# Attention's products with the values: features first, two heads side by side, scaled by spread reciprocals

## The reference, cut to what matters

```
logits = q_lat . c_sel - slope * dist        # masked outside the picked keys
p      = softmax(logits)
o_lat  = p @ c_sel                           # (B, S, 8, 128)
o      = einsum('bshr,hrd->bshd', o_lat, w_uv)   # (B, S, 8, 64), joined to 512 columns
mix    = concat([o, mlstm_out]) @ w_out
```

## Time and profile before

| | us |
|---|---|
| median of 3 runs | 2357.65 |
| lowest, highest | 2354.97, 2359.41 |
| profiled execution, its time | 2356.38 |
| profiled execution, its span | 2354.6 |
| granted TensorE clock, mean over the span | 0.981 |

### The profile page before, as it was taken

The page is one execution under the profiler, slowest core; times in us unless marked ns, Lnnn a source line. Parts: engine busy times, 40 slices in busy tenths (PEclk is TensorE's granted clock), DMA queues, the critical chain, the costliest instruction groups (busy, mean ns, idle before and its releaser), DMA issues.

```text
span 2354.6 us, 35457 instructions
## 1 busy us (share of the span) xinstructions
PE 2254.9 (96%) x10615; PEld 1674.4 (71%) x10616; DVE 1707.5 (73%) x2859; ACT 1338.3 (57%) x1719; POOL 359.9 (15%) x231
## 2 busy tenths in 40 slices
PE   8999998889999999999999999999999999999992
PEld 3644446667755678888888877888787787888872
DVE  0387794745445667778978699787979979778797
ACT  0368723555312555656766577566757757556575
POOL 0000941200020211101201031021103103011030
PEclk9999998989999999999999999999999999999996
DMA  4100002000322967688988799687979979868795
GB/s 178 72 5 36 1 0 90 1 1 1 135 85 94 284 205 231 230 305 292 346 289 303 237 336 365 229 320 240 370 230 346 359 229 346 280 225 306 230 341 208
DMA packets 81676, 493.47 MB, mean 210 GB/s; under 512 B 12307, under 2 KB 13587, under 8 KB 30515
## 3 DMA queue, kind: packets, MB, share of 16 engines
q1 hardware_dynamic: 67344, 451.11, 52.2%
q0 software_dynamic: 12592, 38.29, 7.0%
q10 hardware_dynamic: 1686, 3.37, 0.5%
HBM read 462.31 MB, written 37.88 MB: 212 GB/s over the span
## 4 chain that ended last, share of the span: by engine, by line
PE 66%; DVE 14%; issue 11%; ACT 4%; DVEq 3%; DMA 1%; ACTq 0%; POOL 0%; POOLq 0%; SPq 0%
DVE wlo L1594 8%; PE ps L890 7%; PE ps L888 7%; PE ps L889 7%; PE ps L571 6%; PE ps L885 6%; PE ps L886 6%; PE ps L582 5%; PE ps L762 5%; PE ps L866 3%; PE ps L745 2%; DVEq L408 2%; PE ps L726 2%; ACT whi L1136 2%; PE ps L733 1%
## 5 line engine op out<-in xcount | busy, mean ns | idle before, releaser
L1594 DVE TENSOR_TENSOR wlo<-raw,whi 128x2048 fp32r<-128x2048 f32 x388 | 886.2, 2288 | 248.8 <-ACT whi L1136 205.9
L1136 ACT ACTIVATE whi<-raw 128x2048 fp32r<-128x2048 f32 x388 | 743.1, 1916 | 331.8 <-PE ps L890 331.2
L890 PE MATMUL ps<-whi,xlo 128*128 128x512 f32 x1024 | 399.7, 390 | 0.0
L889 PE MATMUL ps<-wlo,xhi 128*128 128x512 f32 x1024 | 399.6, 390 | 0.0
L888 PE MATMUL ps<-whi,xhi 128*128 128x512 f32 x1024 | 399.2, 390 | 0.0
L1904 POOL DMA_INDIRECT acc<-ysb,idx_cur x45 | 87.6, 1947 | 966.8 <-DVE ysb L1742 593.8
L889 PEld LDWEIGHTS ps<-wlo,xhi 128*128 128x128 f32 x1024 | 192.3, 188 | 40.3
L890 PEld LDWEIGHTS ps<-whi,xlo 128*128 128x128 f32 x1024 | 192.3, 188 | 40.2
L888 PEld LDWEIGHTS ps<-whi,xhi 128*128 128x128 f32 x1024 | 192.5, 188 | 39.2
L888 PE MATMUL ps<-whi,hhi 128*128 128x512 f32 x512 | 206.7, 404 | 0.0
L890 PE MATMUL ps<-whi,hlo 128*128 128x512 f32 x512 | 200.6, 392 | 0.0
(11 more groups left out here) (333 smaller groups left out, 3346.1 us busy)
## 6 DMA issues: line engine op xcount, KB each, us to landing
raw<-in_w_gu SPq DMA_DIRECT2D x260, 1024.0 KB, 6.8
raw<-in_w_dn SPq DMA_DIRECT2D x128, 1024.0 KB, 5.7
raw<-in_w_out SPq DMA_DIRECT2D x2, 2048.0 KB, 9.3
h1all<-in_x SPq DMA_DIRECT2D x4, 1024.0 KB, 8.6
hext<-h1all SPq DMA_DIRECT2D x8, 512.0 KB, 2.6
acc<-h1all SPq DMA_DIRECT2D x8, 512.0 KB, 3.6
fin<-acc SPq DMA_DIRECT2D x4, 1024.0 KB, 8.5
out<-fin SPq DMA_DIRECT2D x8, 512.0 KB, 2.6
```

Source lines behind the costliest of these rows:

```text
L889: pe.matmul(bank_ap, hi, wlo[slot][:, col, :], start=False, stop=False)
L890: return pe.matmul(bank_ap, lo, whi[slot][:, col, :], start=False, stop=stop)
L1136: act.activation(whi[j % 2][:, 4 * g:4 * g + 4, :], raw[:, (j + 2) % 3, 4 * g:4 * g + 4, :], ACT.Copy)\
L1594: dve.tensor_tensor(wlo[j % 2][:, s, :], raw[:, (j + 2) % 3, s, :], whi[j % 2][:, s, :].bitcast(f32), ALU.subtract).then_inc(lo_done, 1)
```

## The change

The products with the values change sides: a head's V (64 columns) becomes the stationary operand and its transposed weights the moving one, so the result has features on partitions. The two heads of a pair write to partitions 0 to 63 and 64 to 127 of the same columns of `ps[NB]`, which puts them on two column halves of the array. They are issued alternately, key tile by key tile, at odd n, for heads n-3 and n-2. `pT` has four buffers instead of two, at another address.

The reciprocals are taken one step earlier. PE spreads them with products of the reciprocals' column (repeated 64 times as the stationary operand) and the identity, so that every partition of a head holds the reciprocals of all 128 tokens; ACT copies them to `recT`. DVE multiplies the collected output by `recT` straight into `catT`. The transposes of `ao` and `ao` itself are gone.

```diff
@@ task_order()
-        if n >= 11 and n % AH == 3:
+        if n > AH and n % AH == 1:
             o += [("at", n // AH - 1)]
@@ tiles
-        pT = at("pT", X + 44, [P, 2, NT, P])
-        ao = at("ao", X + 134.5, [P, 512])
+        pT = at("pT", X + 102, [P, 4, NT, P])
+        recT = at("recT", X + 134.5, [P, 4, P])
@@ tensor engine, after the transposes of head n-1
-                if 2 <= n < NT * AH + 2:
-                    t, h = divmod(n - 2, AH)
+                if n > AH and n % AH == 1:
+                    t = n // AH - 1
+                    b = opened(("at", t))
+                    pe.wait_ge(rec_done, t + 1)
+                    for h in range(AH):
+                        lo, m = AD * (h % 2), h // 2
+                        ins = pe.matmul(b[lo:lo + AD, m * P:(m + 1) * P], att_rec[:, h:h + 1].to_broadcast([P, AD]), ident,
+                                        start=True, stop=True)
+                    closes(ins, ("at", t))
+                if 3 <= n < NT * AH + 2 and n % 2:
+                    t, h = divmod(n - 3, AH)
                     if h == 0:
                         copied(pe, ("V", t))
                         if t:
                             pe.wait_ge(o_copied, t)
-                    for g in range(len(groups(t))):
-                        copied(pe, ("T", n - 2, g))
+                    for i in range(2):
+                        for g in range(len(groups(t))):
+                            copied(pe, ("T", n - 3 + i, g))
                     for j in range(t + 1):
-                        ins = pe.matmul(ps[NB][:, h * AD:wide(h)], pT[:, (n - 2) % 2, j, :],
-                                        Vn[:, j, h * AD:wide(h)], start=j == 0, stop=j == t)
-                    if h == AH - 1:
+                        for i in range(2):
+                            ins = pe.matmul(ps[NB][AD * i:AD * i + AD, h // 2 * P:(h // 2 + 1) * P],
+                                            Vn[:, j, (h + i) * AD:(h + i + 1) * AD], pT[:, (n - 3 + i) % 4, j, :],
+                                            start=j == 0, stop=j == t)
+                    if h == AH - 2:
                         ins.then_inc(o_full, 1)
-                if n >= 11 and n % AH == 3:
-                    t = n // AH - 1
-                    b = opened(("at", t))
-                    pe.wait_ge(o_copied, t + 1)
-                    for j in range(4):
-                        ins = pe.transpose(b[:, j * P:(j + 1) * P], ao[:, j * P:(j + 1) * P], ident)
-                    closes(ins, ("at", t))
@@ before mix
+            pe.wait_ge(o_copied, NT)
             for t in range(NT):
-                copied(pe, ("at", t))
                 copied(pe, ("mt", t))
@@ scalar engine (pT's buffer becomes (n - 1) % 4)
-                if n >= 11 and n % AH == 3:
+                if n > AH and n % AH == 1:
                     t = n // AH - 1
                     b = filled(act, ("at", t))
-                    copy_out(("at", t), catT[:, 0:4, t * P:(t + 1) * P], b[:, :].rearrange("p (j q) -> p j q", q=P))
+                    if t:
+                        act.wait_ge(o_copied, t)
+                    copy_out(("at", t), recT[:, :, :], b[:, :].rearrange("p (j q) -> p j q", q=P))
@@ vector engine (pT's buffer becomes (n - 1) % 4)
-                if n >= 9 and n % AH == 1:
+                if n and n % AH == 0:
+                    t = n // AH - 1
+                    dve.wait_ge(p_ready, AH * (t + 1))
+                    if t:
+                        filled(dve, ("at", t - 1))
+                    dve.reciprocal(att_rec[:, :], att_sum[:, t % 2, :]).then_inc(rec_done, 1)
+                if n > AH and n % AH == 2:
                     t = n // AH - 1
                     dve.wait_ge(o_full, t + 1)
-                    dve.wait_ge(p_ready, AH * (t + 1))
-                    astep(dve.reciprocal(att_rec[:, :], att_sum[:, t % 2, :]))
-                    if t:
-                        filled(dve, ("at", t - 1))
-                    dve.tensor_tensor(ao[:, :].rearrange("p (h d) -> p h d", h=AH),
-                                      ps[NB][:, :].rearrange("p (h d) -> p h d", h=AH),
-                                      att_rec[:, :].unsqueeze(2).to_broadcast([P, AH, AD]), ALU.mult).then_inc(o_copied, 1)
+                    copied(dve, ("at", t))
+                    dve.tensor_tensor(catT[:, 0:4, t * P:(t + 1) * P], ps[NB][:, :].rearrange("p (j q) -> p j q", q=P),
+                                      recT[:, :, :], ALU.mult).then_inc(o_copied, 1)
```

More of the change, by code:

```diff
@@ L357, in layer_kernel @@
             sem("mvar_done"), sem("mroot"), sem("mnorm_in"), sem("mnormed"), sem("mout"))
-        att_shift, p_ready, o_full, o_copied, att_step = (
-            sem("att_shift"), sem("p_ready"), sem("o_full"), sem("o_copied"), sem("att_step"))
+        att_shift, p_ready, o_full, o_copied, rec_done = (
+            sem("att_shift"), sem("p_ready"), sem("o_full"), sem("o_copied"), sem("rec_done"))
         ln_step, ln_var, ln_root, h1_done = sem("ln_step"), sem("ln_var"), sem("ln_root"), sem("h1_done")
@@ L710, in _ @@
                 closes(ins, ("mt", c))
-            def wide(h):
-                return min(h + 2, AH) * AD
             for n in range(2):
@@ L1088, in _ @@
                     b = filled(act, ("T", n - 1, 0))
-                    copy_out(("T", n - 1, 0), pT[:, (n - 1) % 2, j0:j1, :],
+                    copy_out(("T", n - 1, 0), pT[:, (n - 1) % 4, j0:j1, :],
                              b[:, 0:(j1 - j0) * P].rearrange("p (j q) -> p j q", q=P))
-                if n >= 11 and n % AH == 3:
+                if n > AH and n % AH == 1:
                     t = n // AH - 1
                     b = filled(act, ("at", t))
-                    copy_out(("at", t), catT[:, 0:4, t * P:(t + 1) * P], b[:, :].rearrange("p (j q) -> p j q", q=P))
+                    if t:
+                        act.wait_ge(o_copied, t)
+                    copy_out(("at", t), recT[:, :, :], b[:, :].rearrange("p (j q) -> p j q", q=P))
             act.dma_start(lnp[:, 0, :], a["ln1_g"].partition_broadcast(P)).then_inc(lnp_in, 16)
@@ L1511, in _ @@
                       ("mt", c))
-            astep = serial(dve, att_step)
             for n in range(NT * AH + 4):
@@ L1530, in _ @@
                         b = filled(dve, ("T", n - 1, g))
-                        frees(dve.tensor_copy(pT[:, (n - 1) % 2, j0:j1, :],
+                        frees(dve.tensor_copy(pT[:, (n - 1) % 4, j0:j1, :],
                                               b[:, 0:(j1 - j0) * P].rearrange("p (j q) -> p j q", q=P)), ("T", n - 1, g))
-                if n >= 9 and n % AH == 1:
+                if n and n % AH == 0:
[5 more added lines that the diff above has]
+                if n > AH and n % AH == 2:
                     t = n // AH - 1
                     dve.wait_ge(o_full, t + 1)
-                    dve.wait_ge(p_ready, AH * (t + 1))
-                    astep(dve.reciprocal(att_rec[:, :], att_sum[:, t % 2, :]))
-                    if t:
-                        filled(dve, ("at", t - 1))
-                    dve.tensor_tensor(ao[:, :].rearrange("p (h d) -> p h d", h=AH),
-                                      ps[NB][:, :].rearrange("p (h d) -> p h d", h=AH),
-                                      att_rec[:, :].unsqueeze(2).to_broadcast([P, AH, AD]), ALU.mult).then_inc(o_copied, 1)
+                    copied(dve, ("at", t))
+                    dve.tensor_tensor(catT[:, 0:4, t * P:(t + 1) * P], ps[NB][:, :].rearrange("p (j q) -> p j q", q=P),
+                                      recT[:, :, :], ALU.mult).then_inc(o_copied, 1)
             lstep = serial(dve, ln_step)
```

## The result

The changed kernel takes 2367.54 us in the median of its first 8 executions (2357.79 to 2369.11), against 2357.16 for the kernel before beside it: ratio 1.0028, 95% interval 1.0019 to 1.0038. In a second comparison, 10 executions, the median is 2359.74, ratio 1.0017 (1.0004 to 1.0030). The medians differ because its executions fall into two groups: of 18, ten lie between 2355.84 and 2361.86 us with a mean granted clock of 0.982 to 0.984, eight between 2367.49 and 2369.11 with 0.977. The kernel before shows no such gap (2352.58 to 2361.59 in 21 executions). The change makes it slower by 0.2 to 0.3%.

A forecast was written before the change was run, and what follows sets the result against it. The prediction took the exponential's latency, plus transposes and one head's value products, to set each pair in the attention; its terms summed to +1.7 us, 2358.1, and with 1.27 for the median gave 2359.5, range 2353 to 2376.

The forecast's parts named there:

- rival C: First attention tiles: 1.2 GHz lasts through tiles 2 and 3, taking the saving back; 2364 to 2376, chance 0.15.
- the sum: All terms added over the kernel: 2.5 - 1.3 + 3.0 - 2.7 - 1.7 + 1.9 = +1.7 us.
- The sign named for C: In the attention's first tiles, a granted clock of 0.50 past 497 us would show the slow clock lasting.
- Products with the values: Attention, tiles 0 to 5: halved products leave the pair's period unmoved, since PE already waited for the exponential: 0 us.
- Rival B: Attention's value products: column halves don't run side by side, so they double behind the wait; +39 us, 2397, chance 0.17.
- Tiles 7 and 6: Attention's last tiles: the engine-bound part goes, 0.27 us in three pairs of tile 7, 0.17 in three of 6: -1.3.
- Shape changes: Each of 32 head pairs gets one more change of tile shape, transposes to value products: +2.5 us (0 to 6).
- Spread products: On PE's path in each tile: 0.87 us added, 0.44 of transposes removed; +0.43 for 7 tiles, +3.0 us.
- The end: Attention's end before the projection: one value-product time and the transposes with copy go, spread products come: -2.7 us.
- The projection's clock: Output projection's start: PE idles less before it, so the 3.41 us at 1.2 GHz go: -1.7 us.
- The clock in the first tiles: Attention, tile 1: less PE work delays the return to 2.4 GHz, two pairs at 0.94: +1.9 us (-2 to +20).

The follow-up runs named there:

- first profile: The changed kernel unaltered, an execution of its slower group, profiled at 2368.09 us.
- second profile: The changed kernel run again unaltered, an execution of its faster group, profiled at 2355.84 us.
- experiments 1 and 2: Three extra identity products before PE's waits for the exponential, tiles 0 to 2: in the changed kernel 2351.17 us, in the kernel before 2348.81 us.
- Experiment 3: The changed kernel with all value products of a pair's first head issued, then all of the second's: 2386.05 us, ratio 1.0119.
- experiment 4: The changed kernel with the pair's value products and the spread products moved to even steps, before the wait for the exponential: 2327.18 us, ratio 0.9875.
- experiment 6: The changed kernel with extra identity products in tiles 0 to 2 and each tile's spread products issued twice: 2355.15 us, ratio 0.9997.

## Why the prediction was right, and where it was not

The forecast was no change that can be told, 2359.5 in a range of 2353 to 2376; all 18 executions lie in it. Ten average 2358.4, 1.1 below the forecast; eight average 2367.9, which is rival C (middle 2370, chance 0.15). The first median fell on C: +10.4 us, where the sum said +1.7. It is in the range because the range took C in, and whether a median of eight shows the one group or the other is luck. The sign named for C, 1.2 GHz past 497 us, stands in the first profile (503.18) and not in the second (481.90).

Stage and projection together, without what differs elsewhere, are 2.4 us longer in the second profile and 7.8 in the first. The 2.4 lie near the sum's 1.7 partly because errors cancel. At an equal clock the stage alone grows by 3.5 us (experiments 1 and 2), where the sum's terms for it, clock left out, give 2.5 - 1.3 + 3.0 - 2.7 = 1.5; in the faster group the clock term of 1.9 was nothing. Two slips are in the working: the terms of the end give -2.5, not -2.7, and 2358.1 + 1.27 is 2359.4.

- **Products with the values, 0 us in tiles 0 to 5.** Right, and shown: T(n) starts at the same distance from L, AV takes one head's former time, and PE waits 38.4 us where it waited 10.2. Experiment 3 lengthens the AV pair behind the wait, experiment 4 moves it in front, and the pair of heads follows both times as the theory says. Rival B (halves not side by side) is refuted by the 1.90 us of the 32 passes, against 3.25 in turn.
- **Tiles 7 and 6, -0.27 and -0.17 us a pair.** T(n) now starts 0.27 us sooner in tile 7 (4.37 for 4.64), but from there to the next L it takes 2.92 us for 2.75, with the shape change in it, so a pair gains 0.10.
- **Shape changes, +2.5.** From T's last pass to the next product's first it takes 0.203 us where 0.109 was usual, 0.09 more at 2.4 GHz, in 32 pairs about 3.
- **Spread products, +0.43 a tile net.** Right: 0.87 a tile by experiment 6, less the four transposes. With the shape changes, tiles 3 to 6 each last 0.6 to 1.0 us longer.
- **The end, -2.7.** Mis-sized: from the last L to the projection 12.99 us (642.43 - 629.44) for 14.69, -1.7. The timeline of all engines at the stage's end:

```profile
636.73 1.09 PE L729 MATMUL ps<-consts,Lp 128*128 128x128 f32 x8
...
637.86 0.69 DVE L1532 COPY pT<-ps 128x512 f32<-128x512 f32 x1 [2.23 <-PE ps L729]
638.47 0.19 DVE L1539 RECIPROCAL att_rec<-att_sum 128x8 f32<-128x8 f32 x1
...
638.80 1.09 PE L738 MATMUL ps<-consts,att_rec 128*64 128x128 f32 x16 [0.98 <-DVE att_rec L1539]
639.70 1.95 PE L752 MATMUL ps<-pT,Vn 128*64 128x128 f32 x32
...
641.68 0.69 DVE L1544 TENSOR_TENSOR catT<-ps,recT 128x512 f32<-128x512 f32 x1 [3.02 <-PE ps L752]
642.43 0.70 PE L762 MATMUL ps<-raw,catT 128*128 128x512 f32 x1 [0.78 <-DVE catT L1544]
```

The last reciprocal is queued on VectorE behind the copy of T(63)'s second group, and PE stands 0.98 us before the spread products. I had named what the reciprocal would delay and not what would delay it.
- **The projection's clock, -1.7.** Right: no 1.2 GHz there, and the projection takes 1.64 us less.
- **The clock in the first tiles, +1.9.** The step that failed in the slower group. In the faster one it is about 0: 17.1 us at 1.2 GHz as before, and 42.52 - 40.49 = +2.0 us for three tiles is what 12 shape changes (1.1) and two tiles' spread products (0.9) come to. In the slower one the stretch ran to 503.18, into tile 2, and cost 5.3 us more. Rival C had the mechanism and set its end later, in tile 3; I gave 0.15 to what happens in 8 of 18 executions.

## What to carry to other kernels

Before making an engine's work shorter, look at what ends the wait in front of it: work behind a wait for a latency sets the period by its length, work in front of it is free until the gap is full, so move the instructions first and speed them up second. Halving the work of a PE that already waits can cost its clock, in some executions and not in others, so price the stretch at both levels. When added work makes a kernel faster, see in a profile where the time went: half of it can be somewhere else. When a step moves to another engine's queue position, ask both whom it delays and what it now stands behind.

## What the runs showed of the hardware that was not expected

Work that computes nothing made both kernels faster: with 72 extra passes in PE's waits the clock stayed at 2.4 GHz in the three tiles that hold them, 4.1 us less in the kernel before, and a pause of 2.6 us in the experts' loop, 300 us later, was gone with the slow stretch behind it, 4.6 us less. Together they are nearly the 9 us between the medians (2348.81 for 2357.68); what the pause waits for is not known. And by the starts of the records PE began the second head's passes on the free column half while three passes of the first head, issued earlier, were not yet started. So runs as short as tile 1's needed no interleaving by hand: at 1.2 GHz, 8 passes in turn took as long as 8 alternated (pairs of 4.31 and 4.30 us).
